# Start of the experts: two weight loads wait for expert 0's gather, ten unread products in place of 24, and a later place for two modulation pieces on VectorE

## What is computed

```python
y = y + gt1 * o                                        # output projection, gated
h = rms_norm(y, g_ffn[l]) * (1 + sc2) + sh2            # modulated norm
# moe(h): router scores -> best group of four -> top 2 of it -> weights w
hg = jnp.einsum('nd,edf->nef', t, w_gate)              # 16 experts, 1024 x 512 each
hu = jnp.einsum('nd,edf->nef', t, w_up)
a = jax.nn.silu(hg) * hu * gate[..., None]
y = jnp.einsum('nef,efd->nd', a, w_down)               # 512 x 1024 each
```

## Time and profile before

| | |
|---|---|
| median of 3 runs | 1150.08 us (1149.22 to 1152.48) |
| profiled execution | 1151.39 us |
| its span, first to last instruction | 1149.4 us |
| mean granted clock of TensorE | 0.977 |
| TensorE busy | 1076.3 us, 94% |
| VectorE busy | 851.3 us, 74% |
| ScalarE busy | 689.6 us, 60% |
| GpSimd busy | 153.1 us, 13% |
| DMA | 319.86 MB, mean 278 GB/s |

### The profile page before, as it was taken

How to read it: one execution, slowest core, us unless ns; L and a number is a source line. 1 busy time by engine, 2 the same in 40 slices (tenths; PEclk the granted TensorE clock), 3 DMA queues, 4 the chain that set the end, 5 groups by cost and what they waited for, 6 DMA issues and landing times.

```text
span 1149.4 us, 16080 instructions
## 1 busy us (share of the span) xinstructions
PE 1076.3 (94%) x5979; PEld 846.3 (74%) x5981; DVE 851.3 (74%) x1191; ACT 689.6 (60%) x866; POOL 153.1 (13%) x184
## 2 busy tenths in 40 slices
PE   6999989897999999999989998799799999999996
PEld 4798454683788888888869975477378888888885
DVE  5345656667799888888965456766778988889896
ACT  2333555544577778777724365654357777777764
POOL 0326100320011111111040011000001111111002
PEclk8999999998999999999989999999899999999998
DMA  9997889258589999999698381005768999999951
GB/s 348 341 341 218 326 289 296 56 188 347 212 334 371 365 375 368 380 379 381 229 364 244 129 253 58 1 1 196 312 236 314 371 382 369 376 379 371 372 203 57
DMA packets 82560, 319.86 MB, mean 278 GB/s; under 512 B 22464, under 2 KB 26926, under 8 KB 69692
## 3 DMA queue, kind: packets, MB, share of 16 engines
q1 hardware_dynamic: 67232, 285.58, 67.8%
q0 software_dynamic: 14160, 30.19, 7.7%
q10 hardware_dynamic: 1100, 3.23, 0.7%
HBM read 308.05 MB, written 30.57 MB: 295 GB/s over the span
## 4 chain that ended last, share of the span: by engine, by line
PE 79%; issue 7%; DVE 6%; ACT 4%; DMA 3%; SPq 1%; POOL 0%; DVEq 0%; ACTq 0%; POOLq 0%
PE bank L1211 16%; PE bank L1203 15%; PE bank L1204 15%; PE bank L921 3%; PE bank L917 3%; PE bank L914 3%; PE bank L1259 3%; PE bank L1094 2%; PE bank L891 2%; PE bank L1108 2%; ACT work L1601 2%; DMA ring<-in_w_in 2%; PE bank L986 2%; PE bank L1126 2%; PE bank L1027 1%
## 5 line engine op out<-in xcount | busy, mean ns | idle before, releaser
L1661 ACT ACTIVATE work_r<-ring 128x4096 fp32r<-128x4096 f32 x94 | 341.6, 3634 | 126.9 <-PE bank L1204 100.1
L2236 DVE TENSOR_TENSOR ring_r<-ring,work_r 128x4096 fp32r<-128x4096 f32 x92 | 403.9, 4416 | 0.0
L1203 PE MATMUL bank<-work_r 128*128 128x512 f32 x768 | 306.2, 399 | 3.2 <-issue 2.9
L1204 PE MATMUL bank<-work_r 128*128 128x512 f32 x768 | 301.1, 392 | 0.0
L1211 PE MATMUL bank<-ring_r,work_r 128*128 128x512 f32 x768 | 195.2, 396 | 4.2 <-DVE ring_r L2236 4.2
L1211 PEld LDWEIGHTS bank<-ring_r,work_r 128*128 128x128 f32 x768 | 144.2, 189 | 37.4 <-DVE ring_r L2236 5.0
L1203 PEld LDWEIGHTS bank<-work_r 128*128 128x128 f32 x768 | 145.3, 189 | 33.9 <-issue 2.9
L1204 PEld LDWEIGHTS bank<-work_r 128*128 128x128 f32 x768 | 145.0, 189 | 29.0
L2498 POOL DMA_INDIRECT work<-hscr,idx x32 | 36.0, 1125 | 377.4 <-PE bank L1259 266.1
L1517 ACT ACTIVATE work_r<-ring 128x512 fp32r<-128x512 f32 (+1 forms) x48 | 28.8, 603 | 71.8 <-PE bank L921 71.7
L1935 DVE TENSOR_TENSOR ring_r<-ring,work_r 128x512 fp32r<-128x512 f32 (+1 forms) x48 | 32.1, 676 | 50.7 <-ACT work_r L1517 50.6
(11 more groups left out here) (268 smaller groups left out, 1538.9 us busy)
## 6 DMA issues: line engine op xcount, KB each, us to landing
ring<-in_w_gate SPq DMA_DIRECT2D x32, 2048.0 KB, 10.1
ring<-in_w_up SPq DMA_DIRECT2D x32, 2048.0 KB, 10.6
ring<-in_w_down SPq DMA_DIRECT2D x32, 2048.0 KB, 10.6
ring<-in_w_ada SPq DMA_DIRECT2D x24, 2048.0 KB, 10.0
ring<-in_w_in SPq DMA_DIRECT2D x4, 2048.0 KB, 15.1
yscr<-hT POOLq DMA_DIRECT2D x2, 3072.0 KB, 13.0
ring<-yscr SPq DMA_DIRECT2D x6, 1024.0 KB, 7.2
ring<-in_w_out SPq DMA_DIRECT2D x4, 1280.0 KB, 6.9
```

What stands on the lines that cost most here:

```text
L1203: mm(b[:], x_hi[:, k, :], hi[:, k, half, :], start=(k == 0), stop=False)
L1204: last = mm(b[:], x_lo[:, k, :], hi[:, k, half, :], start=False, stop=False)
L1661: A_(w_hi[:, slot % 2, :], ring[slot][:], ACT.Copy).then_inc(s_hi, 1)
L2236: tt(ring_r[slot][:], ring[slot][:], w_hi[:, slot % 2, :].bitcast(F32), ALU.subtract).then_inc(s_lo, 1)
```

## The change

SyncE's extra wait ahead of w_down 0 is now for the landing of expert 0's gather (the semaphore of even experts' gathers, 16 above its value at the layer's start) instead of the landing of the three stores of rows. The unread products ahead of `tokens(0)` are ten in each layer instead of 24. In layer 0 VectorE does B18 and B19 after `onehots(1)`, `onehots(2)` and the second half of `first_expert_low`, not ahead of them. In layer 1 `route[3]` is empty, and its pieces of `route[2]` stay where they are.

```diff
@@ SyncE, stream, step
                             if p == 0 and isinstance(i, int) and (e, kind) == (1, 2):
-                                sp.wait_ge(s_hscr, 16 * NT * (l + 1))
+                                sp.wait_ge(gathers(l, 0)[0][0], gathers(l, 0)[1][0] + 16)
@@ TensorE, experts
                     if p == 0:
                         jobs_done()
 
-                        for _ in range(24):
+                        for _ in range(10):
                             mm(bG[:], onesb[:], swab[:], start=True, stop=True)
@@ VectorE, experts
                     onehots(0)
                     slots(0)
                     if p == 0:
-                        for j in route[2] if l else route[3]:
+                        for j in route[2] if l else []:
                             ada(l, j)
                     if p:
                         rest(0, 0, 0)
@@
                         onehots(q)
                     if p == 0:
                         first_expert_low(1).then_inc(s_lo, 1)
+                        for j in route[3]:
+                            ada(l, j)
```

## The result

The changed kernel takes 1145.08 us (median of 10 runs, 1143.11 to 1147.46), the kernel before in the same comparison 1151.66 us (median of 10, 1147.90 to 1157.35). The ratio is 0.994, with a 95% interval of 0.9924 to 0.9956. Between the medians lie 6.6 us; the forecast's sum was 6.4. Its median, 1143.7 us with a range of 1140.6 to 1147.5, was counted from 1150.1 us for the kernel before, which took 1.6 us more here. A second comparison, with other runs of both, gave 1144.23 against 1152.22 us, a ratio of 0.9928 (0.9905 to 0.9951), 8.0 us between the medians.

What follows compares the result with a forecast made beforehand. TensorE, busy 94% of the span, was taken as the bound, with idle or unread work at each layer's experts' start. Gains of 4.8 (layer 1) and 1.6 us (layer 0) made 6.4: 1150.1 to 1143.7 us, range 1140.6 to 1147.5.

Steps and rivals of the forecast that it cites:

- Layer 1, 4.8 us forecast: Layer 1's experts' start: earlier gather and ten unread products bring expert 0's first product 4.8 us earlier, bounds 2.8 to 5.9.
- Reading the count: Layer 1, before expert 0's first product: TensorE reads VectorE's count; bounded by 0 and 0.5 us, taken as 0.
- a price for each load beside the gather: Expert 0's gather: 9.40 us with two loads beside it, 5.3 with one, 3.2 and 4.2 with none.
- rival C: Expert 0's gather: loads slow it only by bandwidth share, 1.7 us; 3.3 us gained, 1146.8; chance 0.13 shared with another rival.
- Layer 0, 1.6 us forecast: Layer 0's experts' start: 2.3 us gained if the clock holds, 0.1 if it falls, loss about 2.0 if low throughout; 1.6 taken.
- Part 3: Layer 0, B18 and B19 moved later on VectorE: unread products start some 0.7 us later.
- Its check of VectorE: Layer 0: VectorE free from about 277.5, B19 out at 283.9, then nothing more before the tokens.
- The fall behind the 2.08 us idle of layer 1: Layer 1, eight products after the idle: 3.31 instead of 2.12 us; whole fall cost 1.6 us, counted zero with 1.6 either way.
- A: Rival: both clocks hold and layer 1's later fall is missed; 8.7 us gained, 1141.4; chance 0.14.
- B: Rival: the clock falls or stays low in both layers' experts' starts; 2.9 us gained, 1147.2; chance 0.15.
- D: Rival: VectorE's onehots delay layer 1's gather, TensorE idles five us, clock falls; 4.9 us slower, 1155.0; chance 0.06.
- The cover of the loads: Layer 1, delayed weight loads: they land 15 us before ScalarE, their first reader, needs them, so the wait costs nothing.

Runs made afterwards that it cites:

- one load ahead: Changed kernel, but w_down of expert 0 is issued at the old wait and only w_gate of expert 2 waits for the gather; ratio 0.9925 to the kernel before.
- wait alone: Kernel before with only SyncE's new wait for the gather, keeping 24 unread products and the old VectorE order; ratio 0.9963 to the kernel before.
- six products ahead: Changed kernel with six unread products ahead of layer 0's wait for B18 and B19, none behind it; ratio 0.9904 to the kernel before.
- wait and ten: Kernel before with SyncE's new wait and ten unread products, B18 and B19 not moved on VectorE; ratio 0.9968 to the kernel before.
- late loads: Changed kernel with SyncE's wait moved to TensorE's end of expert 0's w_gate, loads some 10 us later; ratio 0.9928 to the kernel before.
- six ahead again: Second run of the changed kernel with six unread products ahead of layer 0's wait and none behind it; ratio 0.9920 to the kernel before.

## Why the prediction was right, and where it was not

**Layer 1, 4.8 us forecast, 4.91 measured.** Each step holds. The landing was put at 3.55 to 4.55 us after the issue and came after 4.39; transposes at 4.36 us behind the gather's issue forecast, 4.43 measured; from there to the first product 2.82 us forecast (0.25 of it for a late clock), 2.66 measured. Reading the count cost nothing that shows. Over the traces with the new wait and ten products layer 1 lies between 8.51 and 9.12 us.

**The reason behind it was only half right.** I read the landings 9.4, 5.3 and 3.2 to 4.2 as a price for each load beside the gather. What counts is how long the loads still run: the gather's first packet is late, then its packets take turns with the loads', and it lands just behind the last of them. For this change both readings give the same number, because no load is ahead any more. For the kernel with one load ahead mine gave 5.3 to 7 and it was 4.7. The forecast also took turns by packet for rival C's rule and set the rule against the 9.4 us. It is another rule: C shares bytes, and its price fails, while the packets of the earlier trace rows's gather do take turns.

**Layer 0, 1.6 us forecast, 0.72 in the first trace.** The two ends (0.1 with a fall of the clock, 2.3 without) hold: 13.56 us is the case with a fall in the longer idle, 11.88 and 11.87 are those without, 2.4 us below 14.28. The two traces of the changed kernel and the two of its variants in SyncE's wait average 12.5, against 14.28 and 13.70 (wait alone, whose layer 0 is as before) for 24 products: about 1.5 us.

**Part 3 was misread.** The forecast priced the pieces' move as 0.7 us of delay and named nothing that it buys. Its check of VectorE took the order after the move, in which VectorE is ready; it never asked what ten products would gain in the old order. There VectorE's onehots and split start only at 283.3 and last until 289.3, so the tokens wait for VectorE whatever TensorE does: 13.97 us without the move. The sum came out right since the sum was made for all three parts together, but a forecast for "the first two parts alone" from the same text would have been 2.7 us too fast in layer 0.

**The falls of the clock.** The fall behind the 2.08 us idle of layer 1, counted at zero with 1.6 us either way, is what nearly all of the table's 1.24 us are. The same idle in the timelines of TensorE of two executions of the changed code, the first trace and then the second:

```profile
854.02 2.13 PE L1211 MATMUL bank<-ring_r,work_r 128*128 128x512 f32 x8 [2.09 <-DVE ring_r L2236]
```

```profile
851.57 3.00 PE L1211 MATMUL bank<-ring_r,work_r 128*128 128x512 f32 x8 [2.09 <-DVE ring_r L2236]
```

After the same 2.09 us the eight products took 2.13 us in one and 3.00 in the other, and from the first product to the end it was 313.46 and 315.02 us. The same code falls in one execution and not in the other. Over all fourteen traces these eight products took 2.66 us or more, a fall, in five in layer 1 and in six in layer 0; of the four with the old wait two fell in layer 1, of the ten others three. So zero with 1.6 us either way fits, and a small gain there is neither shown nor excluded. That a TensorE left idle falls back, as the forecast has it, is not a rule that these traces bear out: after this idle of 2.08 to 2.09 us the clock held in 17 of 28 cases.

**Rivals.** A and B are single outcomes of the clock and were seen in single stretches, not in the median. C's price, an equal share of the bytes, is refuted by the landings table. D's cause is refuted: with the onehots beside it the gather landed after 4.4 us (in layer 0 SyncE issued the waiting load 3.5 us after the gather's issue); its chain was seen where the old wait stayed. The cover of the loads was put at 15 us: w_down of expert 0 landed at 836.1 (10.9 us after its issue, not 8.4) and was read at 848.81, 12.7 us later.

**What stays open.** Why the gather's first packet starts 2.5 us later with two loads ahead of it, what the pieces' move is worth by the medians, and how far the two kernels with six products ahead are below the changed one.

## What to carry to other kernels

Here a gather of some 0.2 MB on the critical chain landed 5 us later because of 4 MB that another queue had issued shortly before it; hold such prefetches back until it has landed, after working out from the reader's row how long they can wait. Unread products paid here only where they ended just as the awaited data came: look at what else the consumer waits for (here VectorE in one layer and a DMA in the other) before cutting or adding them. Price such parts together and in pairs, not one after the other in their final order, or a part that unlocks another looks like pure cost.

## What was not expected of the hardware

Three of the traces have a stretch of granted clock near 0.50 in the attention of layer 1, where the kernel before and the changed kernel have 1.00. The windows of the kernel with the late loads and of the changed one:

```profile
698.00:702.00 4.00, 4.00 (x13) 2.02 (x12) 0.00 (x0) 1.51 (x5) 0.00 (x0) 0.50 0.02 6
```

```profile
698.00:702.00 4.00, 4.00 (x28) 2.47 (x26) 1.51 (x4) 2.65 (x10) 0.00 (x0) 1.00 0.02 4
```

In those three (wait and ten, late loads, six ahead again) the time between the two stretches is 533.84, 535.40 and 533.20 us, in the others 528.97 to 531.61. No part of the change acts there, and of the two traces of the kernel with six products ahead one has the stretch and one has not. So low clock in a stretch of short, dependent products goes with 3 to 5 us more than the others' mean of 530.3, half or more of what this change brings, and a difference of two single executions says little at that size.
